# Squared-ReLU feed forward on one core: inner units by three narrow matmuls per weight block into one PSUM bank, rectified on ScalarE and multiplied with the bank on VectorE

## The reference, cut to what matters

```python
D_MODEL, SEQ, DEPTH, D_FF = 1024, 256, 2, 4 * 1024

def sq_relu_mlp(h, w1, w2):
    return jnp.square(jax.nn.relu(h @ w1)) @ w2
...
    for l in range(DEPTH):
        ...
        x = x + memory_xattn(rms_norm(x, xattn_norm_g[l]), mem_n, xa_w_q[l], xa_w_kv[l], ...)
        x = x + sq_relu_mlp(rms_norm(x, mlp_norm_g[l]), mlp_w1[l], mlp_w2[l])
```

## Time and profile before

| | us |
|---|---|
| median of 3 runs | 1762.71 (1761.33 to 1763.09) |
| profiled execution, its own time | 1759.92 |
| its span in the profile | 1758.6 |
| TensorE busy | 1688.6 (96% of the span) |
| VectorE busy | 1233.5 (70%) |
| ScalarE busy | 892.5 (51%) |
| up stages of the two squared feed forwards | about 249 to 341 and 554 to 646 of the span |

### The profile page before, as it was taken

The page is one execution under the profiler, slowest core; times in us unless marked ns, Lnnn a source line. Parts: engine busy times, 40 slices in busy tenths (PEclk is TensorE's granted clock), DMA queues, the critical chain, the costliest instruction groups (busy, mean ns, idle before and its releaser), DMA issues.

```text
span 1758.6 us, 24398 instructions
## 1 busy us (share of the span) xinstructions
PE 1688.6 (96%) x10133; PEld 1490.4 (85%) x10136; DVE 1233.5 (70%) x1487; ACT 892.5 (51%) x1149; POOL 184.6 (10%) x166
## 2 busy tenths in 40 slices
PE   7979999999999999999999899999999999899997
PEld 6768998888999888888889688888888898688886
DVE  7865667765656777677767758778787667677764
ACT  6544455544545545455544545555555445455542
POOL 0500110011101001100021001003200111010002
PEclk9999999999999999999999899999999999999999
DMA  7333335555433555555554214555555543135551
GB/s 280 138 124 140 127 137 193 192 192 195 167 141 136 195 211 184 192 181 183 201 181 158 91 49 181 183 189 215 178 190 190 194 178 120 48 144 180 185 200 60
DMA packets 41439, 291.09 MB, mean 166 GB/s; under 512 B 4720, under 2 KB 4976, under 8 KB 7024
## 3 DMA queue, kind: packets, MB, share of 16 engines
q1 hardware_dynamic: 39456, 282.61, 44.6%
q10 hardware_dynamic: 1872, 6.92, 1.0%
HBM read 288.46 MB, written 1.05 MB: 165 GB/s over the span
## 4 chain that ended last, share of the span: by engine, by line
PE 82%; DVE 11%; ACT 4%; issue 2%; POOL 1%; DMA 0%; ACTq 0%; DVEq 0%; POOLq 0%
PE ps L298 36%; PE ps L297 18%; PE ps L295 4%; DVE w_lo L1399 4%; PE ps L286 3%; PE ps L288 3%; PE ps L287 3%; PE ps L331 3%; PE ps L333 3%; PE ps L332 3%; PE ps L296 2%; DVE xT L1407 2%; ACT w_hi L888 1%; POOL stat L2054 1%; PE ps L437 1%
## 5 line engine op out<-in xcount | busy, mean ns | idle before, releaser
L1399 DVE TENSOR_TENSOR w_lo<-raw,w_hi 128x2048 fp32r<-128x2048 f32 x268 | 613.6, 2293 | 232.1 <-ACT w_hi L888 228.2
L298 PE MATMUL ps<-xT,w_hi 128*128 128x512 f32 x1736 | 619.7, 396 | 0.0
L888 ACT ACTIVATE w_hi<-raw 128x2048 fp32r<-128x2048 f32 x268 | 510.1, 1904 | 215.1 <-PE ps L298 117.7
L297 PE MATMUL ps<-xT,w_lo 128*128 128x256 f32 x1736 | 485.0, 279 | 0.0
L298 PE MATMUL ps<-hT,w_hi 128*128 128x512 f32 x1168 | 412.5, 397 | 0.0
L298 PEld LDWEIGHTS ps<-xT,w_hi 128*128 128x128 f32 x1736 | 326.4, 188 | 67.4
L297 PEld LDWEIGHTS ps<-xT,w_lo 128*128 128x128 f32 x1736 | 327.9, 189 | 11.5
L297 PE MATMUL ps<-hT,w_lo 128*128 128x256 f32 x1168 | 327.1, 280 | 1.7 <-DVE hT L1584 1.7
L298 PEld LDWEIGHTS ps<-hT,w_hi 128*128 128x128 f32 x1168 | 219.3, 188 | 50.9
L297 PEld LDWEIGHTS ps<-hT,w_lo 128*128 128x128 f32 x1168 | 220.3, 189 | 5.0 <-DVE hT L1584 2.9
L940 ACT ACTIVATE tmp<-ps 128x512 f32<-128x512 f32 x120 | 71.7, 598 | 257.6 <-PE ps L298 257.6
(11 more groups left out here) (254 smaller groups left out, 2068.7 us busy)
## 6 DMA issues: line engine op xcount, KB each, us to landing
raw<-weights_dram SPq DMA_DIRECT2D x264, 1024.0 KB, 4.8
raw<-weights_dram SPq DMA_DIRECT2D x4, 768.0 KB, 4.1
tmp<-mem_dram ACTq DMA_DIRECT2D x2, 1024.0 KB, 7.0
x<-x_in_dram SPq DMA_DIRECT2D x2, 512.0 KB, 5.6
raw<-weights_dram SPq DMA_DIRECT2D x2, 512.0 KB, 6.5
arena<-mem_dram ACTq DMA_DIRECT2D x1, 1024.0 KB, 7.9
arena<-pool_mat_dram ACTq DMA_DIRECT2D x1, 1024.0 KB, 4.8
tmp<-masks_dram ACTq DMA_DIRECT2D x1, 768.0 KB, 8.3
```

Source lines behind the costliest of these rows:

```text
L297: pe.matmul(ps[:, bank, 0:S], lo, src[:, k, 0, :], start=False, stop=False)
L298: return pe.matmul(ps[:, bank, :].rearrange("p (a n) -> p a n", a=2), hi, src[:, k, :, :], start=False, stop=last)
L888: act.activation(b.w_hi[:, s, 0:w], b.raw[:, s, 0:w], ACT.Copy).then_inc(*mark("hi", u))
L1399: dve.tensor_tensor(b.w_lo[:, s, 0:w], b.raw[:, s, 0:w], b.w_hi[:, s, 0:w].bitcast(F32), ALU.subtract).then_inc(*mark("lo", u))
```

## The change

TensorE works the up units of the two squared feed forwards with `head_unit` instead of `up_unit`. The result of up unit j now lies complete in one bank (bank 0 or bank 2). ScalarE writes max(value, 0) of the whole bank to `tmp` where it copied the right halves. VectorE multiplies the bank by that, which is one instruction where there were an addition and a rectified product. A bank is now free after `h32` of the unit two before, and the buffer in `tmp` as well. The down units, the gated feed forwards and all the rest stay as they are.

```diff
@@ feed_forward in tensor_program
             for j in range(n):
                 if j >= 2:
-                    pe.wait_ge(*at("z", f, j - 2))
-                up_unit(u + j, 2 * (j % 2), f if j == 0 else None)
+                    pe.wait_ge(*at("h32", f, j - 2))
+                head_unit(u + j, 2 * (j % 2), f if j == 0 else None)
@@ feed_forward in scalar_program
             else:
-                second_half(u + j, b.hid(j % 2), 2 * (j % 2), f, j, ("z", f, j - 2) if j >= 2 else None)
+                act.wait_ge(*at("unit", u + j))
+                if j >= 2:
+                    act.wait_ge(*at("h32", f, j - 2))
+                act.activation(b.hid(j % 2), b.pair(2 * (j % 2)), ACT.Relu).then_inc(*mark("half", f, j))
                 highs(u + j + 3)
@@ feed_forward in vector_program
             else:
-                z, h32 = b.hid(2 + j % 2), b.hid(4 + j % 2)
-                halves_sum(z, b.hid(j % 2), 2 * (j % 2), "z", f, j)
-                dve.wait_ge(*at("z", f, j))
+                h32 = b.hid(4 + j % 2)
+                dve.wait_ge(*at("half", f, j))
                 if j >= 2:
                     dve.wait_ge(*at("hhi", f, j - 2))
-                dve.scalar_tensor_tensor(h32, z, 0.0, z, ALU.max, ALU.mult).then_inc(*mark("h32", f, j))
+                dve.tensor_tensor(h32, b.pair(2 * (j % 2)), b.hid(j % 2), ALU.mult).then_inc(*mark("h32", f, j))
```

## The result

| | before | changed |
|---|---|---|
| median of 9 runs | 1762.70 us (1759.92 to 1768.41) | 1770.49 us (1763.35 to 1774.42) |
| profiled execution | 1759.92 us, span 1758.6 | 1767.41 us, span 1766.1 |

The ratio is 1.0040 with a 95% interval of 1.0028 to 1.0053, so the change costs 4.9 to 9.3 us, about 7.1 (the medians differ by 7.8). Forecast were 4.9 us. The changed kernel's runs spread over 11 us, those of the kernel before over 8.5.

The account below looks back on a forecast made before the run. TensorE's own pitch was taken to bound the up stage. Only its narrow tiles counted, +4.9 us, all else 0: 1762.71 + 4.9 = 1767.6 us, slower by 0.28%, range 1764.4 to 1770.2 us.

Parts of the forecast that it names:

- Step 1: TensorE's up units: narrow tiles in place of wide ones cost 0.165 us more per unit, on 30 units, +4.9 us.
- Unit 0's share: Up unit 0's 0.165 us go into TensorE's wait before unit 1, which shrinks from 1.32 to about 1.15 us.
- Rival 1: Narrow matmuls in the up stage cost 0.117 us, as in wide tiles, so time stays at 1762.7 us; chance 12%.
- Steps 2 to 4: Up units: ScalarE's Relu for copy, VectorE's one instruction less (23 us freed), TensorE's new wait for `h32`; 0 each.
- rival 2: Second-stack mixers, throttled clock: first escapes its longer drop, 1766.0 us, or second gets one, 1769.2; chance 25%, split evenly.

## Why the prediction was right, and what it missed

**What bounds the stage.** Right. TensorE is busy 70.00 of 70.00 us before and after.

**Step 1, 0.165 us per unit on 30 units.** Right: 0.167, 5.0 us. Reading the price from a stream of the same matmuls elsewhere in the program gave the pitch within 0.002 us (5.758 against 5.760), and the experiment with three matmuls in the old layout shows that it is the number of matmuls alone, each with its weight load. Of the page "TensorE: Matmul & The Clock Gate" of the Trainium skill, the section "Back-to-back issue gap" would have given an estimated 1.2 us; three kernels show four times that. The section states this rule for isolated matmuls and says that in a stream with weight loads both set the spacing, a condition that the prediction left out. Unit 0's share went into the wait as said, which shrank by 0.10 us, not 0.17. Rival 1, the narrow matmul at the wide pair's price, is refuted.

**Steps 2 to 4.** Right: Relu 0.60, product 0.69, idle time 1.11, no wait for `h32` (TensorE is busy 70.00 of 70.00 us), and the relief of VectorE worth nothing, shown by giving it back.

**The sum.** It fell short. Its mechanism was right and a term was missing. The sum took all the code outside the up stages as unchanged, and rival 2 took the clock in the mixers as a toss with equal weight up and down and 1.6 us at most. Both were wrong: in the four kernels whose mixers start 5 us later the clock brings 1.2 to 2.4 us more on average (1.6 to 3.3 us more of missing clock time, at 0.74), and a single long low stretch costs up to 8.5 us, five times what the comparison of the two layers in the earlier trace rows could show. One profile holds two samples of such an event and sets no upper end. The range held only at its edge: the ratio of 1.0040 on the time before gives 1769.8, the median of 1770.49 lies 0.3 us above it, and single runs reach 1774.4. That it held is in part luck, and it was too narrow on that side.

**The chances.** Slower by more than 0.2% was the likeliest case and came, with 5.0 us of the 7.1 from the cause that was named.

## What to carry to other kernels

Price an extra matmul by a stream of the same shape in the same trace, not by its columns: here three of 256 columns cost 0.360 us where 512 and 256 cost 0.350. Work taken off an engine that waits anyway only lengthens its wait. When a change delays code that runs at a varying clock, compare runs at an equal clock, or hold the clock, before a difference is put down to the change; and look whether filling idle places of TensorE brings back more than it costs. Here it gave 0.25% by the ratio, 4.4 us (3.8 by medians), nearly what the change took from its own stage.

## What the runs showed of the hardware that was not expected

- TensorE's weight loads are busy 70.00 of 70 us in the narrow stream and 61.00 in the wide one, while the matmuls are 0.120 us apart. The loads' records are 0.19 us long each and start 0.12 us apart, so they overlap, as in this timeline of the changed kernel:

```profile
256.67 0.19 PEld L287 LDWEIGHTS ps<-xT,w_lo 128*128 128x128 f32 x1
...
256.79 0.19 PEld L288 LDWEIGHTS ps<-xT,w_hi 128*128 128x128 f32 x1
```

  That the loads set the 0.120 us is a reading, not shown: in every kernel here a third matmul per block comes with a third load.
- The same eight matmuls of 256 columns behind an idle place take 3.78 us, or 1.89 when small matmuls fill that place: the granted clock is at its lower level (1.2 GHz, 0.50 by the window) after the idle time and at the upper (2.4 GHz, 1.00 over the filled mixer) after the filled one.
- The same stretch of code takes 109.4 to 117.9 us from run to run by the clock alone, and with a delay of 5 us ahead of it the share of runs with a mean clock of 0.984 or less was 44% in place of 14%. The cause of this is open: of the five profiles that hold a mixer of 117.9 us four come from kernels with a delay in front of it (2.5, 5.0, 5.0 and 8.1 us) and one from the kernel with the fillers behind it.
